# Later mixers: the third quarter of projection F right behind the scores of head step 8

## The chip, the cores and the metric

One Trainium2 chip, one core of it. The metric is the device time of one execution in microseconds (us); the median of three runs is compared. The engines have the profile's names: PE (TensorE), DVE (VectorE), ACT (ScalarE), POOL, SP. PEld is the weight load of a product.

## The reference, cut to what matters

The program computes two model blocks, one after the other, on 256 tokens of width 1024. The first is a gated linear attention, convolution and differential attention mixer with a mixture of experts. The second has two layers, each of them a feed-forward network, a token mixer and a feed-forward network:

```python
for l in range(DEPTH_2):                      # 2 layers
    x = x + 0.5 * gate0 * swiglu(h, ffn_w13[l, 0], ffn_w2[l, 0])
    x = x + gate1 * token_mixer(h, w_in[l], ..., w_out[l], cos, sin)
    x = x + 0.5 * gate2 * swiglu(h, ffn_w13[l, 1], ffn_w2[l, 1])

# token_mixer: proj = h @ w_in; three mixers of 64-wide heads, joined, @ w_out
s_cmp = einsum('bgrsd,bgcd->bgrsc', qg, kcmp) * scale     # 15 compressed keys, 8 heads
p_cmp = masked_softmax(s_cmp, cmp_mask)
o_cmp = einsum('bgrsc,bgcd->bgrsd', p_cmp, vcmp)
o     = g[..., 0:1] * o_cmp + g[..., 1:2] * o_slc + g[..., 2:3] * o_win   # heads 0 to 7
p     = masked_softmax(s + forget bias, causal)            # heads of the forgetting mixer
```

The change touches the token mixer alone, and so it acts twice in one execution, in layer 0 and in layer 1.

## The kernel before

Each engine runs a list of instructions that is written out by hand (`mixer_pe`, `mixer_act`, `mixer_dve`, `mixer_sp`, `mixer_pool`). There is no scheduler: an engine takes its list in order, and a `wait_ge` holds everything that stands behind it on that engine. Each engine has one counter; `done(key)` raises it and remembers the count, and `wait_ge(*P(key))` waits until PE's counter has that count (A is ACT's, V is DVE's).

**Projections.** The mixer's input projection is cut into blocks A to F. A block has two halves of the inner dimension (weight units `u(x, half)`) and two tiles of 128 tokens. `chunk(x, half, t)` is one quarter of a block, 12 products of 512 columns (L544, L545, L550) into bank 6 + t of `ps`. The order of the quarters is (0,0), (0,1), (1,0), (1,1), so `chunk("F", 1, 0)` is the third: the second half of the weights, on the first tile of tokens. It waits for the upper parts `whi` of its unit (ACT, L337) and the lower parts `wlo` (DVE, L344). `ahead_act(n0 + k)` and `ahead_dve(n0 + k)` make the parts of unit n0 + k + 3; block F's second half is unit n0 + 15, which `ahead_act(n0 + 12)` and `ahead_dve(n0 + 12)` make.

**Head steps.** Twelve steps `g` of two heads each go through the same stations: `scores(g)` on PE (L2473, L2483, in steps 8 and 9 L2479 too), `maxima(g)` on DVE (L2890, L2891, L2893), `exps(g)` on ACT (L2711), `norm(g)` on both (DVE L2902/L2903 or L2905, then L2909; ACT L2721), `turned_probs(g)` on PE (six transposes, L2491), `probs(g)` on both (ACT L2732, DVE L2915), `values(g)` on PE (L2503), and `emit(g)` on DVE (L2924). "The ninth head step" is g = 8.

**Compressed attention.** Its keys `KC` come from DVE (L3039, L3042). PE multiplies them with the queries in eight small f32 products of 32 columns (L2627, sixteen rows in the trace; key `cs`) into bank 5. DVE then masks (L3052), takes maxima and subtracts (L3055 to L3057), ACT takes the exponential (L2834), DVE sums and divides (L3065 to L3070, key `cp`), and PE turns the result (L2639).

On DVE, behind the scores of step 8, stand in this order: `maxima(8)`, `probs(7)`, the wait for `cs` with L3052 to L3057, `norm(8)`, `ahead_dve(n0 + 14)` (one L344), `emit(7)`, `maxima(9)`, `probs(8)`, L3065 to L3070. On ACT: `exps(8)`, `probs(7)`, `norm(8)`, L2834, `ahead_act(n0 + 15)`, `exps(9)`.

Of the kernel before, what the change touches and what calls it, by code (L numbers as in the profile page):

```python
# [140 lines left out]
class Kernel:  # L141
# [2233 lines left out]
    def mixer_pe(self, pe, l):  # L2375
# [5 lines left out]
        def chunk(x, half, t, free=None):  # L2381

            if half == 0:
                pe.wait_ge(*free)
            mm = self.proj_mm(pe, st, u(x, half), half, t, ps[:, 6 + t, 0:512], 512, False)
            if t == 1:
                mm.then_inc(*P.done("unit", u(x, half)))
                P.at["pj", st, x, 1] = P.n
            elif half == 1:
                mm.then_inc(*P.done("pj", st, x, 0))  # L2390
# [73 lines left out]
        def scores(g):  # L2464
            r = g % 2
            if g >= 2:
                pe.wait_ge(*A("pc", st, g - 2))
                pe.wait_ge(*V("pc", st, g - 2))
            heads = [self.mixer_heads(g, i) for i in range(2)]
            fox = g in (8, 9)  # L2470
            for qt in range(2):
                for i, (q, k, _) in enumerate(heads):
                    pe.matmul(ps[:, 2 * r + i, 128 * qt:128 + 256 * qt], q(qt), k(qt + 1), start=qt == 0, stop=False)  # L2473
            if fox:
                pe.wait_ge(*self.G("nFb", st))
                for qt in range(2):
                    for i in range(2):
                        h = 32 * (2 * (g - 8) + i)
                        pe.matmul(ps[:, 2 * r + i, 128 * qt:128 + 256 * qt], self.oneb[h:h + 3],  # L2479
                                  self.nFb[h:h + 3, 0:128 + 128 * qt], start=False, stop=False)  # L2480
            for i in range(2):
                for c in (0, 256):
                    mm = pe.matmul(ps[:, 2 * r + i, c:c + 128], self.identb, self.trib, start=False, stop=c == 256)  # L2483
            mm.then_inc(*P.done("sc", st, g))

        def turned_probs(g):
            r = g % 2
            for i in range(2):
                pe.wait_ge(*(A if i == 0 else V)("an", st, g))
                for c in range(3):  # L2490
                    mm = pe.transpose(ps[:, 2 * r + i, c * 128:c * 128 + 128], self.apb[:, r, i, c * 128:c * 128 + 128], ident)  # L2491
                mm.then_inc(*P.done("pt", st, g, i))

        def values(g):
            r = g % 2
            pt = self.apt[:, r, :, :]
            if g >= 1:
                pe.wait_ge(*V("em", st, g - 1))
            pe.wait_ge(*A("pc", st, g))
            pe.wait_ge(*V("pc", st, g))  # L2500
            for t in range(2):
                for i in range(2):
                    mm = pe.matmul(ps[64 * i:64 * i + 64, 4, 128 * t:256], self.mixer_heads(g, i)[2](t), pt[:, i, 256 * t:256 + 128 * t],  # L2503
                                   start=t == 0, stop=t == 1)
            mm.then_inc(*P.done("pv", st, g))
# [114 lines left out]
        values(6)  # L2620

        scores(8)
        pe.wait_ge(*V("KC", st))
        for t in range(2):
            for j in range(4):
# [1 line left out]
                mm = pe.matmul(ps[:, 5, 32 * (4 * t + j):32 * (4 * t + j) + 32], pj[:, t, c:c + 128],  # L2627
                               v["KC"].rearrange("p g c -> p (g c)"), start=True, stop=True)
        mm.then_inc(*P.done("cs", st))
        turned_probs(7)  # L2630
        chunk("F", 1, 0)
        values(7)

        scores(9)
# [758 lines left out]
```

## Time and profile before

| | |
|---|---|
| median of 3 runs | 1444.89 us (1444.31 to 1445.31) |
| profiled execution: its time, and its span | 1444.9 us, 1444.9 us |
| PE busy | 1397.9 us, 97% of the span |
| DVE busy | 1150.0 us, 80% |
| ACT busy | 791.6 us, 55% |
| the changed place, layer 0 | about 679 to 694 us |
| the changed place, layer 1 | about 1203 to 1217 us |

Span and time are the same here, so a time worked out in the trace stands for the measured one. PEclk in the rows below is the clock that TensorE was granted, as a share of 2.4 GHz: 0.50 is 1.2 GHz. A row of the timeline gives start, duration to the end of the last instruction of the group, engine, line, operation, tiles, shape and count, and in square brackets the engine's idle time before it with what ended it. Products are pipelined, so the step from one row's start to the next row's start tells more than a row's duration.

### The profile page before, as it was taken

Reading aid. Unit: us, or ns where it says so; the run is one execution under the profiler, and the core shown is the slowest. Engines: PE = TensorE matmul, PEld = TensorE weight load, DVE = VectorE, ACT = ScalarE, POOL = GpSimd, SP = SyncE. Lnnn points to the kernel's source line nnn. Section 1 sums busy time; section 2 is a strip of 40 time slices with the busy share of each in tenths; the row PEclk is TensorE's granted clock in tenths of the full one; section 3 lists DMA queues with packets and bytes.
Section 4 is the critical chain, followed back from the end, with each engine's and each line's share of the span. In section 5 each row is a group of like instructions: output and inputs, shape, how many; then the busy total and the mean of one; then the engine's idle time right before and its main releaser. Section 6 shows DMA issues by size and latency. Waiting matters only on the chain. (4 is left out here: it accounts for less than half of the span.)

```text
span 1444.9 us, 20189 instructions
## 1 busy us (share of the span) xinstructions
PE 1397.9 (97%) x7974; PEld 1188.8 (82%) x7974; DVE 1150.0 (80%) x1605; ACT 791.6 (55%) x1163; POOL 38.1 (3%) x47
## 2 busy tenths in 40 slices
PE   8998999999999999998999999999999989999997
PEld 6886888998788888777788888888888777888886
DVE  6797788889789987877778987898888787777653
ACT  7546545764456542767565543555535667655541
POOL 0021000000000000100000000000000100000000
PEclk9999999999999999999999999999999999999999
DMA  9123366998666878534347869677786433376450
GB/s 361 59 88 110 132 253 254 351 368 311 236 248 250 339 284 324 199 133 164 117 158 301 336 240 345 247 292 318 283 311 259 169 137 119 118 303 221 177 202 29
DMA packets 58110, 330.34 MB, mean 229 GB/s; under 512 B 6752, under 2 KB 7312, under 8 KB 28560
## 3 DMA queue, kind: packets, MB, share of 16 engines
q1 hardware_dynamic: 56400, 325.93, 59.8%
q10 hardware_dynamic: 1616, 3.12, 0.6%
q8 instruction: 64, 1.05, 0.3%
q14 instruction: 30, 0.25, 0.0%
HBM read 327.95 MB, written 1.07 MB: 228 GB/s over the span
## 5 line engine op out<-in xcount | busy, mean ns | idle before, releaser
L344 DVE TENSOR_TENSOR wlo<-raw,whi 128x2048 fp32r<-128x2048 f32 (+2 forms) x236 | 533.8, 2265 | 87.9 <-ACT whi L337 86.7
L337 ACT ACTIVATE whi<-raw 128x2048 fp32r<-128x2048 f32 (+2 forms) x236 | 445.9, 1894 | 134.7 <-PE ps L1622 87.5
L1374 PE MATMUL ps<-hreg_r,whi 128*128 128x512 f32 x1504 | 359.5, 391 | 1.9 <-ACT whi L337 0.8
L1374 PEld LDWEIGHTS ps<-hreg_r,whi 128*128 128x128 f32 x1504 | 276.6, 188 | 56.4 <-ACT whi L337 1.0
L385 DVE CUSTOM_DVE_ANT_0 adaw<-adaw,crow,colp 128x1024 f32<-128x1024 f32 x144 | 182.5, 1280 | 39.7 <-DMA adaw<-in_wada 39.4
L1383 PEld LDWEIGHTS ps<-hreg_r,wlo 128*128 128x128 f32 x1504 | 192.5, 191 | 7.0
L1383 PE MATMUL ps<-hreg_r,wlo 128*128 128x256 f32 x1504 | 195.6, 283 | 0.0
L1551 ACT ACTIVATE mix<-ps 128x512 f32<-128x512 f32 x93 | 55.6, 598 | 213.6 <-PE ps L1383 213.6
L1614 PE MATMUL ps<-whi,ireg_r 128*128 128x512 f32 x416 | 129.5, 392 | 1.1 <-ACT ireg_r L1508 1.1
L1618 PE MATMUL ps<-wlo,ireg_r 128*128 128x512 f32 x416 | 128.2, 389 | 0.0
L1622 PE MATMUL ps<-whi,ireg_r 128*128 128x512 f32 x416 | 128.2, 389 | 0.0
L544 PE MATMUL ps<-whi,hreg_r 128*128 128x512 f32 (+2 forms) x288 | 114.4, 401 | 3.0 <-ACT whi L337 1.3
L545 PE MATMUL ps<-whi,hreg_r 128*128 128x512 f32 (+2 forms) x288 | 108.7, 382 | 0.0
L1557 DVE TENSOR_TENSOR mix<-ps,mix 128x512 f32<-128x512 f32 x93 | 64.2, 690 | 51.2 <-ACT mix L1551 50.1
L1622 PEld LDWEIGHTS ps<-whi,ireg_r 128*128 128x128 f32 x416 | 78.0, 188 | 16.5 <-DVE ireg_r L1562 0.2
L1618 PEld LDWEIGHTS ps<-wlo,ireg_r 128*128 128x128 f32 x416 | 78.1, 188 | 16.3
L1614 PEld LDWEIGHTS ps<-whi,ireg_r 128*128 128x128 f32 x416 | 77.1, 188 | 17.1 <-ACT ireg_r L1508 1.8
L550 PE MATMUL ps<-wlo,hreg_r 128*128 128x512 f32 (+2 forms) x288 | 73.6, 378 | 0.4 <-DVE wlo L344 0.4
L544 PEld LDWEIGHTS ps<-whi,hreg_r 128*128 128x128 f32 x288 | 55.1, 191 | 14.2 <-ACT hreg_r L479 2.9
L2711 ACT ACTIVATE ireg<-ps,an 128x128 f32<-128x128 f32 x96 | 39.1, 419 | 43.1 <-DVE an L2893 43.1
L545 PEld LDWEIGHTS ps<-whi,hreg_r 128*128 128x128 f32 x288 | 55.2, 192 | 8.5
L550 PEld LDWEIGHTS ps<-wlo,hreg_r 128*128 128x128 f32 x288 | 52.5, 190 | 11.7 <-DVE wlo L344 1.7
(416 smaller groups left out, 1740.6 us busy)
## 6 DMA issues: line engine op xcount, KB each, us to landing
raw<-in_wu SPq DMA_DIRECT2D x182, 1024.0 KB, 5.8
adaw<-in_wada SPq DMA_DIRECT2D x144, 512.0 KB, 5.1
raw<-in_wx SPq DMA_DIRECT2D x48, 1024.0 KB, 6.2
greg<-gates SPq DMA_DIRECT2D x6, 512.0 KB, 6.7
raw<-in_wu SPq DMA_DIRECT2D x4, 568.0 KB, 5.9
raw<-in_wu SPq DMA_DIRECT2D x2, 544.0 KB, 5.3
x<-in_x SPq DMA_DIRECT2D x2, 512.0 KB, 4.2
out<-hreg SPq DMA_DIRECT2D x2, 512.0 KB, 2.6
```

Of the source, the lines that this page charges most:

```text
L337: act.activation(self.whi[:, m, 0:width], self.raw[:, n % NRAW, 0:width], ACT.Copy).then_inc(*self.A.done("hi", n))
L344: dve.tensor_tensor(self.wlo[:, m, 0:width], self.raw[:, n % NRAW, 0:width], self.whi[:, m, 0:width].bitcast(F32), ALU.subtract).then_inc( ...
L385: dve.tensor_tensor_reduce(w, w, self.crow, 1.0, self.col("bada")[:, n:n + 1], ALU.mult, ALU.add, self.mod2[:, n:n + 1]).then_inc(*self.V. ...
L544: pe.matmul(bank, self.hhi[:, kt, tk], wh, start=kt == 0, stop=False)
L545: pe.matmul(bank, self.hlo[:, kt, tk], wh, start=False, stop=False)
L550: mm = pe.matmul(bank, self.hhi[:, kt, tk], self.wlo[:, m, i * width:i * width + width], start=False, stop=kt == 7)
L1374: pe.matmul(self.ps[:, b, :], self.whi[:, m, c:c + 128], self.hboth[:, kt], start=kt == 0, stop=False)
L1383: mm = pe.matmul(self.ps[:, b, 0:256], self.wlo[:, m, c:c + 128], self.hhi[:, kt, :], start=False, stop=kt == 7)
L1557: dve.tensor_tensor(to, self.ps[:, b:b + 2, 0:256], to, ALU.add).then_inc(*self.V.done("sum", st, nth, part))
L1614: pe.matmul(self.ps[:, b, :], hidden(k, t)[0], weights(self.whi, k), start=first and k == 0, stop=False)
L1618: pe.matmul(self.ps[:, b, :], hidden(k, t)[0], weights(self.wlo, k), start=False, stop=False)
L1622: mm = pe.matmul(self.ps[:, b, :], hidden(k, t)[1], weights(self.whi, k), start=False, stop=last and k == 1)
```

## The change

`chunk("F", 1, 0)` and `turned_probs(7)` are written ahead of the wait for `KC` and the eight small products, where they stood behind them; among themselves they change places too.

```diff
         scores(8)
+        chunk("F", 1, 0)
+        turned_probs(7)
         pe.wait_ge(*V("KC", st))
         for t in range(2):
             for j in range(4):
                 c = MIXC["B"][0] + 128 * j
                 mm = pe.matmul(ps[:, 5, ...], pj[:, t, c:c + 128],
                                v["KC"].rearrange("p g c -> p (g c)"), start=True, stop=True)
         mm.then_inc(*P.done("cs", st))
-        turned_probs(7)
-        chunk("F", 1, 0)
         values(7)
 
         scores(9)
```

The order on PE, as a difference of the two programs (minus: before, plus: after; layer 0). First the place behind the scores of step 8 (L2479, L2483), with the small products L2627 and the transposes L2491 that leave it, and the first rows of the F quarter (L544, L545).

```order
 L2479 MATMUL ps<-nFb,greg_b 128x256 x2
 L2483 MATMUL ps<-bm 128x128 x4
-L2627 MATMUL ps<-rs,ireg 128x32 [waits dve_result]
-L2627 MATMUL ps<-rs,ireg 128x32 x7
-L2491 MATMUL ps<-cst,ireg 128x128 [waits act_result]
-L2491 MATMUL ps<-cst,ireg 128x128 x2
-L2491 MATMUL ps<-cst,ireg 128x128 [waits dve_result]
-L2491 MATMUL ps<-cst,ireg 128x128 x2
 L544 MATMUL ps<-whi,hreg_r 128x512 [waits act_result]
 L545 MATMUL ps<-whi,hreg_r 128x512
```

The F quarter now follows the scores with nothing between. Next the place behind the F quarter (its last rows are L550) and ahead of `values(7)` (L2503); the small products are L2629 in the changed file.

```order
 L550 MATMUL ps<-wlo,hreg_r 128x512 [waits dve_result]
 L550 MATMUL ps<-wlo,hreg_r 128x512 x3
+L2491 MATMUL ps<-cst,ireg 128x128 [waits act_result]
+L2491 MATMUL ps<-cst,ireg 128x128 x2
+L2491 MATMUL ps<-cst,ireg 128x128 [waits dve_result]
+L2491 MATMUL ps<-cst,ireg 128x128 x2
+L2629 MATMUL ps<-rs,ireg 128x32 [waits dve_result]
+L2629 MATMUL ps<-rs,ireg 128x32 x7
 L2503 MATMUL ps<-ireg 64x256 [waits dve_result,act_result]
 L2503 MATMUL ps<-ireg 64x256
```

The transposes of step 7 come first there, and the small products last. The lists of DVE, ACT, POOL and SP are the same in both programs. This is DVE's list at the same place, from `probs(7)` to `maxima(9)`:

```order
L2915 COPY ireg<-ps 128x384 [waits pe_result]
L3052 TENSOR_TENSOR hreg<-ps,cst 128x128 [waits pe_result]
L3052 TENSOR_TENSOR hreg<-ps,cst 128x128
L3055 TENSOR_REDUCE st<-hreg 128x16 [waits dve_result]
L3056 TENSOR_SCALAR st<-st 128x16 [waits dve_result]
L3057 TENSOR_TENSOR hreg<-hreg,st 128x256 [waits dve_result]
L2905 RECIPROCAL an<-an 128x4 [waits act_result]
L2909 TENSOR_SCALAR ireg<-ireg,an 128x128 [waits dve_result]
L2909 TENSOR_SCALAR ireg<-ireg,an 128x256
L344 TENSOR_TENSOR wlo<-raw,whi 128x2048 [waits act_result]
L2924 TENSOR_TENSOR mix<-ps,mix 128x256 [waits dve_result,pe_result]
L2890 TENSOR_REDUCE an<-ps 128x2 [waits pe_result]
```

Nothing moved in it: L3052 still waits for the small products, and everything down to L2890 still stands behind L3052.

## Rows read from the trace of the kernel before

**Rows 1.** The page's list of engines: busy time, share of the span, instructions.

```profile
PE 1397.9 (97%) x7974; PEld 1188.8 (82%) x7974; DVE 1150.0 (80%) x1605; ACT 791.6 (55%) x1163; POOL 38.1 (3%) x47
```

**Rows 2.** Windows: stretch, length, busy times, PEclk, DMA share, GB/s; both layers.

```profile
677.80:681.20 3.40, 2.86 (x31) 2.08 (x27) 3.30 (x11) 2.67 (x11) 0.00 (x0) 1.00 0.65 214
681.20:688.00 6.80, 6.80 (x24) 5.83 (x24) 4.97 (x13) 5.50 (x14) 0.00 (x0) 0.50 0.27 112
...
1203.40:1206.80 3.40, 2.86 (x26) 2.69 (x24) 2.88 (x11) 2.67 (x5) 0.00 (x0) 1.00 0.82 279
1206.80:1210.20 3.40, 3.40 (x9) 2.62 (x8) 3.26 (x10) 3.35 (x14) 0.00 (x0) 0.50 0.09 34
```

**Rows 3.** Timeline of PE, layer 0, from the scores of step 8 to L2639.

```profile
679.06 0.40 PE L2483 MATMUL ps<-bm 128*128 128x128 bf16 x4
679.99 2.57 PE L2627 MATMUL ps<-rs,ireg 128*128 128x32 f32 x16 [0.54 <-DVE ireg L3042]
682.37 1.52 PE L2491 MATMUL ps<-cst,ireg 128*128 128x128 f32 x6
...
688.54 0.87 PE L2503 MATMUL ps<-ireg 128*64 128x256 f32 x8
...
690.46 0.40 PE L2483 MATMUL ps<-bm 128*128 128x128 bf16 x4
690.70 0.82 PE L2491 MATMUL ps<-cst,ireg 128*128 128x128 f32 x6
691.28 0.48 PE L544 MATMUL ps<-whi,hreg_r 128*128 128x512 f32 x1
...
694.14 0.44 PE L2639 MATMUL ps<-cst,hreg 128*128 128x128 f32 x2
```

**Rows 4.** Timeline of DVE, layer 0, the same place.

```profile
672.49 2.29 DVE L344 TENSOR_TENSOR wlo<-raw,whi 128x2048 fp32r<-128x2048 f32 x1 [2.75 <-ACT whi L337]
...
679.18 0.76 DVE L3042 TENSOR_TENSOR ireg<-ps,cst 128x256 f32<-128x256 f32 x2
...
680.25 0.55 DVE L2909 TENSOR_SCALAR ireg<-ireg,an 128x128 f32<-128x128 f32 x2
...
683.93 0.56 DVE L2915 COPY ireg<-ps 128x384 f32<-128x384 f32 x1 [1.66 <-PE ps L2491]
684.40 0.48 DVE L3052 TENSOR_TENSOR hreg<-ps,cst 128x128 f32<-128x128 f32 x2
...
685.93 0.17 DVE L2905 RECIPROCAL an<-an 128x4 f32<-128x4 f32 x1
...
686.60 2.28 DVE L344 TENSOR_TENSOR wlo<-raw,whi 128x2048 fp32r<-128x2048 f32 x1
689.45 0.42 DVE L2924 TENSOR_TENSOR mix<-ps,mix 128x256 f32<-128x256 f32 x1 [0.57 <-PE ps L2503]
690.90 0.42 DVE L2890 TENSOR_REDUCE an<-ps 128x2 f32<-128x256 f32 x1 [1.02 <-PE ps L2483]
...
693.66 0.42 DVE L3070 TENSOR_TENSOR hreg<-hreg,st 128x256 f32<-128x256 f32 x1
```

**Rows 5.** Timeline of ACT, layer 0: norm(7), probs(7), norm(8).

```profile
680.25 0.80 ACT L2721 ACTIVATE ireg<-ireg,an 128x128 f32<-128x128 f32 x2 [0.72 <-DVE an L2903]
...
684.35 0.49 ACT L2732 ACTIVATE ireg<-ps 128x384 f32<-128x384 f32 x1
686.13 0.80 ACT L2721 ACTIVATE ireg<-ireg,an 128x128 f32<-128x128 f32 x2 [1.30 <-DVE an L2905]
```

**Rows 6.** Timeline of PE, layer 1, the same place.

```profile
1204.10 1.97 PE L2627 MATMUL ps<-rs,ireg 128*128 128x32 f32 x16 [0.54 <-DVE ireg L3042]
1205.90 0.85 PE L2491 MATMUL ps<-cst,ireg 128*128 128x128 f32 x6
...
1211.03 0.87 PE L2503 MATMUL ps<-ireg 128*64 128x256 f32 x8
...
1216.63 0.44 PE L2639 MATMUL ps<-cst,hreg 128*128 128x128 f32 x2
```

## The prediction

> **What bounds the kernel now.** I read the page's list of engines first: PE is busy 97% of the span [rows 1], so time is to be won where PE stands still, or where it runs slowly while busy. The windows show both at the changed place [rows 2]. From 681.2 to 688.0 us (layer 0) and from 1206.8 to 1210.2 us (layer 1) PE is busy all the time, but at a granted clock of 0.50, that is 1.2 GHz instead of 2.4. In the stretch ahead of each fall PE is busy 2.86 of 3.40 us. The timeline of PE says with what [rows 3]: it stands 0.54 us for the keys KC (DVE L3042, which ends at 679.18 + 0.76 = 679.94), and then issues sixteen small products (L2627). Layer 1 does the same [rows 6].
>
> The timelines of DVE and ACT then say what the place is waiting for once PE is faster [rows 4, 5]. DVE idles 1.66 us ahead of probs(7) (L2915) and 1.02 us ahead of maxima(9) (L2890), both for PE. Thus DVE has slack, but as a sum only 2.7 us in layer 0, and most of it stands ahead of L3052, which waits for the small products.
>
> **The change, step by step, layer 0.** All starts are issue times; a step is the distance of two starts.
>
> PE leaves the scores of step 8 at 679.30: L2483 starts at 679.06, and from L2483 to the next group it takes 690.70 - 690.46 = 0.24 us [rows 3]. Before, L2627 started at 679.99, so 0.69 us of standing goes. What hides the wait for KC now is the F quarter itself: 2.86 us at the full clock (691.28 to 694.14, the fourth quarter of F, same shape [rows 3]). If that cover were gone, the wait would be the old one.
>
> The F quarter needs its weights. The L344 that makes their lower parts ends at 672.49 + 2.29 = 674.78, and it waited for the upper parts [rows 4]: no wait at 679.30. It costs nothing new. It runs 679.30 to 682.16.
>
> The transposes of step 7 follow at 682.16. Their inputs are ready: ACT's half at 680.25 + 0.80 = 681.05, DVE's at 680.25 + 0.55 = 680.80 [rows 4, 5]. They take 691.28 - 690.70 = 0.58 us at the full clock [rows 3], so they issue until 682.74; before, they issued at 682.37 at the low clock.
>
> The small products issue from 682.74. At the full clock they take 1205.90 - 1204.10 = 1.80 us and end 1.97 us behind their start [rows 6]: issue until 684.54, end at 684.71. Their other bound is 2.38 us (679.99 to 682.37), part of it at the low clock [rows 3]. I take 1.80, because a solid F quarter now precedes them; the other end would make everything behind later by 0.6 us.
>
> Here the late step appears. DVE's L3052 waits for them. Before, it started at 684.40 directly behind probs(7). Now probs(7) can start at about 683.0 and is no hindrance, but L3052 starts at 684.75: **0.35 us later**. From L3052 the DVE list is fixed, steps from the rows [rows 4]: L2905 1.53 later at 686.28, L344 2.20 later at 686.95, end 2.28 on at 689.23. emit(7) (L2924) lasts 0.42 us, of which the next group overlaps some 0.1, as behind L2915 (0.56 long, next start 0.47 later). So maxima(9) starts at 689.5 instead of 690.90. Then L3070 ends (693.66 + 0.42) - 690.90 = 3.18 us behind it, at 692.7, and L2639 on PE can start at 692.73 (before 694.14, 0.06 behind L3070).
>
> PE meanwhile: values(7) waits for ACT's probs(7), 684.35 + 0.49 = 684.84 [rows 5], which the move does not make earlier: the row shows no idle time ahead of it, so ACT is busy until then. It starts at 684.88: **0.34 us of waiting**. From values(7) to the transposes of step 8 it takes 690.70 - 688.54 = 2.16 us [rows 3]: 687.04. They wait for norm(8): ACT starts 0.20 behind L2905 and takes 0.80 [rows 4, 5], so 687.28 and a start at 687.33: **0.29 us**. Transposes 0.58, fourth F quarter 2.86: PE is done at 690.77 and waits for L3070 until 692.73: **1.96 us**. Scores 9 end near 687.2 (684.88 + 690.46 - 688.54 + 0.40), long before 689.5, so DVE's list decides, with its L344 of 2.28 us inside.
>
> The sum on PE to L2639: saved are 0.69 (the wait) and the low clock's price. Transposes and F quarter took 688.54 - 682.37 = 6.17 us and need 694.14 - 690.70 = 3.44 at the full clock, 2.73 saved; the small products 2.38 - 1.80 = 0.58. Together 4.00 us. Given back are 0.34 + 0.29 + 1.96 = 2.59 us. **Layer 0: 1.4 us faster.** DVE's chain gives the same: maxima(9) 690.90 to 689.5.
>
> **Layer 1.** The old time is better there, since the low clock lasted only 3.4 us [rows 2]: small products already 1.80, transposes and F quarter 1211.03 - 1205.90 = 5.13 instead of 3.44 [rows 6]. Saved: 0.70 + 1.69 = 2.39. Given back: the same 2.59, because the DVE list is the same. **Layer 1: 0.2 us slower.** In absolute starts, L2639 moves from 1216.63 by -1.4 (layer 0's gain ahead of it) and +0.2, to about 1215.4 [rows 6].
>
> Behind L2639 the order of all lists is the old one and DVE, ACT and PE are shifted alike, so nothing is won or lost until the clock says so. No DMA is issued by the moved rows. Weight parts from `ahead_dve(n0 + 14)` are finished 0.35 us later (layer 0), and they serve a later unit.
>
> Sum: -1.4 + 0.2 = -1.2 us against the profiled execution's 1444.9, which equals the median 1444.89: **1443.7 us**.
>
> **The clock, the large unknown.** The rows show what the low clock costs: 2.73 + 0.58 = 3.3 us where it lasted 6.8 us, 1.7 us where it lasted 3.4 [rows 2, 3, 6]. They show what PE did ahead of a fall: a wait, then small products. The changed order has such places too: small products at 682.7 followed by 0.34 us of waiting, and, worse, the wait of 1.96 us ahead of L2639 followed by small groups (turns, scores). The Trainium skill ("TensorE: Matmul & The Clock Gate", section "Part 1: The HAM clock gate") says that the throttled clock is the default and that activity releases it. By that rule the new wait of about 2 us ahead of L2639 calls for a fall just behind it; the trace agrees in so far as both falls here follow a wait. By the rule the sum would be 1445.4, by the rows' full clock 1443.7.
>
> **The rivals.**
> - Forecast, clock stays full behind the change, DVE's list decides: 1443.7, own range 1443.0 to 1444.5 (0.6 us for the bound of the small products, and the spread of the runs). Chance 0.50.
> - The fall moves instead of vanishing: in one layer the low clock comes behind L2639. For it: the wait grows from nothing to 2 us. Against: two thirds of the place before it is now dense (F quarters). Price 1.7 us (short) or 3.3 us (long): 1445.4 or 1447.0. Chance 0.30, most of it short.
> - No net effect: values(7), norm(8) and the DVE list give all of the gain back, or the small products run at the low clock in both layers (1.2 us): 1444.9. Chance 0.10.
> - Slower: the clock falls behind L2639 in both layers and stays low for the long stretch, 2 x 3.3 = 6.6 us on top: 1450.3. It decides only if the falls together cost over 4.1 us, so one long fall is not enough. Chance 0.06.
> - Faster: the DVE list is not what PE waits for, because L344 or L3052 finds its place earlier, so nothing is given back: 4.0 + 2.4 = 6.4 us, 1438.5. Against it stands the fixed order of DVE. Chance 0.04.
>
> **How the numbers follow.** About 0.2% (2.9 us) is what a measurement here tells from no change. Faster than 1442.0 needs the last case, 0.04. Slower than 1447.8 needs the fourth, 0.06. The rest, 0.90, is within. The range 1443.0 to 1446.5 holds the forecast, the case without effect and the short fall, about 0.8.
>
> **What the changed profile would show.** Right: no idle time of PE ahead of the F quarter behind step 8, its start near 679.3 and its length 2.9 us at a clock of 1.00; L3052 at 684.7; PE waits for DVE L3070 about 2 us ahead of L2639; L2639 near 692.7 in layer 0 and near 1215.4 in layer 1. Wrong: a low clock in 691 to 702 or 1214 to 1225, small products of more than 2 us, or maxima(9) that starts directly behind the scores of step 9.

## The result: slower by 0.2%, outside the range

| | median us | lowest to highest | runs |
|---|---|---|---|
| before | 1445.38 | 1443.19 to 1448.60 | 16 |
| changed | 1449.09 | 1445.69 to 1453.55 | 16 |

The ratio is 1.002, 95% interval 1.0012 to 1.0029: 2.9 us slower, 1.7 to 4.2. The medians themselves lie 3.7 us apart. The forecast was 1443.7 us, with a range of 1443.0 to 1446.5 and a chance of 0.90 for no change beyond 0.2%. A second set of twelve runs of the changed kernel (label e12_after_again, below) gave 1.0017 (1.0006 to 1.0028). Single runs of either kernel differ by 5 to 8 us, which the three runs shown before did not tell. Two runs of the kernel before in one group of the experiments, at 3540 us, are left out of every ratio and mean.

The page's list of engines of the changed kernel answers to [rows 1]; nothing in it tells of the loss.

```profile
PE 1399.0 (97%) x7974; PEld 1190.2 (82%) x7974; DVE 1149.2 (79%) x1605; ACT 790.6 (55%) x1163; POOL 38.1 (3%) x47
```

PE's timeline of the changed kernel, layer 0, answers to [rows 3] (L2629 are the small products). I add L2479, the forgetting part of the scores, as a fixed point: it marks the scores of step 8 in every kernel here. The last row, L456, is the first transpose of the stage behind the mixer.

```profile
678.87 0.34 PE L2479 MATMUL ps<-nFb,greg_b 3*128 3x128 bf16 x4
...
679.35 0.48 PE L544 MATMUL ps<-whi,hreg_r 128*128 128x512 f32 x1
...
682.21 0.81 PE L2491 MATMUL ps<-cst,ireg 128*128 128x128 f32 x6
682.86 1.87 PE L2629 MATMUL ps<-rs,ireg 128*128 128x32 f32 x16
...
687.35 0.88 PE L2491 MATMUL ps<-cst,ireg 128*128 128x128 f32 x6 [0.37 <-ACT ireg L2721]
...
692.72 0.44 PE L2639 MATMUL ps<-cst,hreg 128*128 128x128 f32 x2 [1.76 <-DVE hreg L3070]
...
724.64 1.03 PE L456 MATMUL ps<-cst,hreg 128*128 128x128 f32 x8
```

DVE's timeline of the changed kernel, same place, answers to [rows 4]:

```profile
683.06 0.56 DVE L2915 COPY ireg<-ps 128x384 f32<-128x384 f32 x1 [1.69 <-PE ps L2491]
684.76 0.49 DVE L3052 TENSOR_TENSOR hreg<-ps,cst 128x128 f32<-128x128 f32 x2 [1.15 <-PE ps L2629]
...
686.29 0.17 DVE L2905 RECIPROCAL an<-an 128x4 f32<-128x4 f32 x1
...
686.96 2.28 DVE L344 TENSOR_TENSOR wlo<-raw,whi 128x2048 fp32r<-128x2048 f32 x1
...
689.50 0.41 DVE L2890 TENSOR_REDUCE an<-ps 128x2 f32<-128x256 f32 x1
```

In layer 0 each of these steps stands within 0.15 us of its forecast: the F quarter at 679.35 (679.30), L3052 at 684.76 (684.75), maxima(9) at 689.50 (689.5), L2639 at 692.72 (692.73). In layer 1 the interval from L2479 to L2639 is the same:

```profile
1205.43 0.34 PE L2479 MATMUL ps<-nFb,greg_b 3*128 3x128 bf16 x4
...
1219.28 0.44 PE L2639 MATMUL ps<-cst,hreg 128*128 128x128 f32 x2 [1.76 <-DVE hreg L3070]
```

So 13.85 us in both layers. L2639 of layer 1 was forecast at 1215.4 and stands at 1219.28, 3.9 us later, though the interval is as forecast: the time is lost between the two places. Set beside the first profile of the kernel before, the span is 2.6 us longer (1447.5 against 1444.9): -1.50 us at the place of layer 0, +1.57 behind it (30.35 became 31.92, with the low clock shown below), +2.39 from L456 to L2479 of layer 1 (1202.89 - 724.49 = 478.40 became 1205.43 - 724.64 = 480.79), +0.11 at the place of layer 1, and under 0.1 in each other part. The forecast had nothing for the second and the third of these. What it also lacked is what the unchanged place takes when the clock is full there. The windows of the changed kernel, to be read like [rows 2], show that low clock did not leave:

```profile
659.70:666.50 6.80, 6.11 (x32) 4.86 (x33) 6.59 (x8) 3.93 (x11) 0.00 (x0) 0.50 0.41 154
679.30:692.70 13.40, 11.29 (x80) 8.88 (x78) 10.18 (x28) 9.46 (x25) 0.00 (x0) 1.00 0.37 136
693.90:697.20 3.30, 3.30 (x20) 2.26 (x18) 1.78 (x5) 0.93 (x3) 0.00 (x0) 0.50 0.00 0
```

The changed place itself has the full clock, PE is busy 11.29 of 13.40 us of it, and right behind the new wait the clock is at 1.2 GHz for 3.4 us.

### The profile page after: what moved, and what is told of

Same layout as the page of the kernel before. It is cut to its first block and busy times, and to the rows that moved or that the text cites. A ratio compares the mean times of both kernels' runs of the same rounds, so it can differ in the third digit from the quotient of the medians.

```text
span 1447.5 us, 20189 instructions
## 1 busy us (share of the span) xinstructions
PE 1399.0 (97%) x7974; PEld 1190.2 (82%) x7974; DVE 1149.2 (79%) x1605; ACT 790.6 (55%) x1163; POOL 38.1 (3%) x47
## 3 DMA queue, kind: packets, MB, share of 16 engines
HBM read 327.95 MB, written 1.07 MB: 227 GB/s over the span
## 5 line engine op out<-in xcount | busy, mean ns | idle before, releaser
L344 DVE TENSOR_TENSOR wlo<-raw,whi 128x2048 fp32r<-128x2048 f32 (+2 forms) x236 | 533.4, 2264 | 89.1 <-ACT whi L337 88.0
L544 PE MATMUL ps<-whi,hreg_r 128*128 128x512 f32 (+2 forms) x288 | 112.8, 396 | 3.2 <-ACT whi L337 1.8
L545 PE MATMUL ps<-whi,hreg_r 128*128 128x512 f32 (+2 forms) x288 | 106.9, 375 | 0.0
L550 PE MATMUL ps<-wlo,hreg_r 128*128 128x512 f32 (+2 forms) x288 | 73.0, 375 | 0.4 <-DVE wlo L344 0.4
L544 PEld LDWEIGHTS ps<-whi,hreg_r 128*128 128x128 f32 x288 | 54.2, 188 | 14.2 <-ACT hreg_r L479 2.6
L550 PEld LDWEIGHTS ps<-wlo,hreg_r 128*128 128x128 f32 x288 | 51.7, 188 | 11.4 <-DVE wlo L344 1.7
L545 PEld LDWEIGHTS ps<-whi,hreg_r 128*128 128x128 f32 x288 | 54.2, 188 | 8.2
```

The lines of the kernel that those rows point to most:

```text
L344: dve.tensor_tensor(self.wlo[:, m, 0:width], self.raw[:, n % NRAW, 0:width], self.whi[:, m, 0:width].bitcast(F32), ALU.subtract).then_inc( ...
L544: pe.matmul(bank, self.hhi[:, kt, tk], wh, start=kt == 0, stop=False)
L545: pe.matmul(bank, self.hlo[:, kt, tk], wh, start=False, stop=False)
L550: mm = pe.matmul(bank, self.hhi[:, kt, tk], self.wlo[:, m, i * width:i * width + width], start=False, stop=kt == 7)
```

## The experiments

Three theories. **List**: the small products come later, DVE's fixed list (L3052 to L3057, norm(8), L344, maxima(9), L3070) starts later, and PE waits for its end in each layer. **Clock**: the new wait brings low clock behind it. **DMA**: the loss arises in the later feed-forward stages. Each kernel had 11 or 12 runs. They ran in three groups (e1 to e4, e5 to e8, e9 to e12), each on one chip of its own, and a ratio is taken against the 35 runs of the kernel before on the same chip, whose medians were 1445.9, 1445.9 and 1444.3 us. So across groups the ratios are to be compared, not the medians. The table below is worked out from each profile's starts: L2639 minus L2479 of step 8 (the place), L456 minus L2639 (what is behind it in the mixer). For the first profile of the kernel before, the rows of PE that [rows 3, 6] lack are these, the first for layer 0 and the last for layer 1, and they give 694.14 - 678.79 = 15.35, 724.49 - 694.14 = 30.35 and 1216.63 - 1202.89 = 13.74:

```profile
678.79 0.34 PE L2479 MATMUL ps<-nFb,greg_b 3*128 3x128 bf16 x4
...
724.49 1.03 PE L456 MATMUL ps<-cst,hreg 128*128 128x128 f32 x8
...
1202.89 0.34 PE L2479 MATMUL ps<-nFb,greg_b 3*128 3x128 bf16 x4
```

| kernel | median us | ratio (95%) | place, layers 0 and 1 | behind, layers 0 and 1 |
|---|---|---|---|---|
| before, first profile | 1445.38 | | 15.35, 13.74 | 30.35, 30.37 |
| e5 before again | 1445.04 | 0.9997 (0.9984 to 1.0009) | 13.75, 11.59 | 30.33, 30.33 |
| changed | 1449.09 | 1.0020 (1.0012 to 1.0029) | 13.85, 13.85 | 31.92, 30.32 |
| e12 changed again | 1447.91 | 1.0017 (1.0006 to 1.0028) | 13.85, 13.86 | 30.34, 31.89 |
| e8 layer 0 alone | 1447.37 | 1.0012 (1.0000 to 1.0024) | 13.85, 11.59 | 30.36, 30.36 |
| e1 L344 moved | 1446.58 | 1.0007 (0.9995 to 1.0018) | 11.96, 11.95 | 31.89, 31.89 |
| e6 before, L344 moved | 1448.10 | 1.0016 (1.0005 to 1.0027) | 12.16, 12.16 | 32.04, 33.29 |
| e2 wait filled | 1446.88 | 1.0015 (1.0001 to 1.0028) | 13.86, 13.87 | 30.32, 30.35 |
| e3 transposes last | 1448.42 | 1.0014 (1.0002 to 1.0025) | 14.36, 14.36 | 30.36, 30.36 |
| e10 norm(8) first | 1446.64 | 1.0016 (1.0003 to 1.0029) | 13.67, 13.66 | 31.92, 31.68 |
| e4 F quarter split | 1443.57 | 0.9991 (0.9977 to 1.0005) | 12.51, 12.51 | 30.34, 30.33 |
| e11 the same again | 1445.09 | 0.9994 (0.9981 to 1.0008) | 12.52, 12.52 | 30.36, 30.32 |
| e7 split, L344 moved | 1446.24 | 0.9999 (0.9986 to 1.0012) | 11.77, 11.77 | 32.08, 32.04 |
| e9 before, wait filled | 1445.31 | 0.9997 (0.9986 to 1.0008) | 12.33, 12.33 | 30.36, 30.33 |

**e5, the kernel before again.** No edit.

> The kernel before, unchanged, for a second profile and more runs. In the first profile both layers had low clock at the changed place. Theory List says what it looks like where a layer has the full clock there: small products 1.8 us, PE at L2639 about 11.1 to 11.5 us behind the start of the small products (it was 14.15 and 12.53 us with the low clock), and 1.3 to 1.7 us ahead of the same point of the changed kernel, measured from the scores of step 8. Theory Clock alone says that a layer at the full clock is no faster to L2639 than the changed kernel's.

Its PE timeline of layer 1 is the unchanged order at the full clock:

```profile
1203.31 0.34 PE L2479 MATMUL ps<-nFb,greg_b 3*128 3x128 bf16 x4
1203.82 1.92 PE L2627 MATMUL ps<-rs,ireg 128*128 128x32 f32 x16
...
1214.90 0.44 PE L2639 MATMUL ps<-cst,hreg 128*128 128x128 f32 x2
```

and DVE's:

```profile
1206.94 0.48 DVE L3052 TENSOR_TENSOR hreg<-ps,cst 128x128 f32<-128x128 f32 x2
...
1209.13 2.29 DVE L344 TENSOR_TENSOR wlo<-raw,whi 128x2048 fp32r<-128x2048 f32 x1
...
1211.67 0.42 DVE L2890 TENSOR_REDUCE an<-ps 128x2 f32<-128x256 f32 x1
```

L3052 starts 3.63 us behind L2479; in the changed kernel 684.76 - 678.87 = 5.89. That is 2.26 us, and L2639 is late by the same: 13.85 against 11.59. So the direction is List's, with a larger size than expected (1.3 to 1.7). One reason is that this layer did not even wait for KC: L2627 follows L2479 by 0.51 us, where a wait makes it 1.20 (679.99 - 678.79). The windows of this profile show what may have made PE late enough not to wait:

```profile
682.40:685.80 3.40, 3.40 (x12) 2.83 (x11) 2.50 (x10) 3.02 (x12) 0.00 (x0) 0.50 0.26 106
1184.30:1191.00 6.70, 6.00 (x32) 4.76 (x31) 6.62 (x8) 3.80 (x11) 0.00 (x0) 0.50 0.42 157
1203.30:1214.90 11.60, 11.56 (x87) 8.96 (x85) 10.54 (x30) 9.47 (x25) 0.00 (x0) 1.00 0.48 157
```

Low clock stood some 19 us ahead (1184.3 to 1191.0). That PE came late from there, and so found KC ready, is my reading; e8's layer 1, with no wait either, has 11.59 us too, and the same stretch 19 us ahead of its L2479 at 1201.91:

```profile
1182.80:1189.60 6.80, 6.05 (x32) 4.80 (x31) 6.67 (x8) 3.84 (x11) 0.00 (x0) 0.50 0.45 152
```

So the two intervals of 11.59 us are not free of low clock: its price was paid ahead of L2479, where the table does not count it. An unchanged layer at the full clock that does wait for KC takes longer, as e9 shows below. Layer 0 of e5 had its low clock at the place (682.4), 13.75 us. Where low clock falls changes between runs of one kernel.

**e1 and e6, L344 out of the list.** The same edit on DVE, in the changed kernel and in the kernel before:

```diff
         norm(8)
-        self.ahead_dve(dve, n0 + 14)
 
         emit(7)
         maxima(9)
...
         dve.tensor_tensor(S16, S16, sm..., ALU.mult).then_inc(*V.done("cp", st))
+        self.ahead_dve(dve, n0 + 14)
```

> The changed kernel, with one thing moved: on DVE the L344 that stands between norm(8) and emit(7) comes behind L3070. Theory List: the small products, late by the F quarter, hold L3052 and everything behind it on DVE, and with the 2.28 us of L344 in that list PE waits 1.8 us ahead of L2639 in each layer. Then L2639 comes near 690.9 in layer 0 (692.72 in the changed kernel), the wait ahead of it is under 0.3 us, and the median is 3 to 4 us under the changed kernel's, 1445 to 1446. Theory Clock: what costs is low clock behind that wait. It expects the same direction, as the wait is gone, but with the low clock gone from behind L2639. Theory DMA (the loss arises in the later feed-forward stages, from landings of weights that come at another time): no gain, 1448 to 1450.

> The kernel before, with L344 moved behind L3070 on DVE, as in the experiment on the changed kernel. Theory List: before the change PE hardly waits ahead of L2639, so there is nothing to win: within 1 us of the kernel before, 1445 to 1447. A rival says that the moved L344 alone makes the kernel faster, with or without the change: then 1442 to 1444.

PE of e1, layer 0:

```profile
678.74 0.34 PE L2479 MATMUL ps<-nFb,greg_b 3*128 3x128 bf16 x4
...
690.70 0.38 PE L2639 MATMUL ps<-cst,hreg 128*128 128x128 f32 x2
693.64 0.87 PE L2491 MATMUL ps<-cst,ireg 128*128 128x128 f32 x6 [1.07 <-ACT ireg L2721]
```

The wait ahead of L2639 is gone and the place takes 11.96 us, 1.9 less, as List says: DVE's list set the 13.85. But the stretch behind takes 31.89 instead of 30.3 in both layers, at the full clock: L344 now holds norm(9), and PE waits for that (1.07 us ahead of the transposes of step 9). So the edit gives back most of what it wins: place and rest are 43.85 against 44.2 us. Its ratio is 1.0007 against the changed kernel's 1.0020, some 1.9 us less, more than these 0.35 us per layer; the rest may be low clock (see "The mean granted clock" below) or spread. The median, 1446.58, lies above the 1445 to 1446 expected. e6 shows the other side: in the kernel before the move takes away next to nothing and costs the same 1.7 us behind, 0.16% slower (layer 1 also has low clock behind the place, 33.29). I had expected no difference there. Its PE list is that of the kernel before, so it gives two more layers of the unchanged order on PE. Both wait for KC, and neither has low clock at the place. This is the wait in layer 0, and the window of that place:

```profile
680.49 1.97 PE L2627 MATMUL ps<-rs,ireg 128*128 128x32 f32 x16 [0.55 <-DVE ireg L3042]
```

```profile
679.30:691.40 12.10, 11.55 (x86) 8.97 (x84) 9.40 (x33) 10.16 (x29) 0.00 (x0) 1.00 0.25 91
```

**e2, the wait filled.** On PE, in the changed kernel:

```diff
         chunk("F", 1, 1)
+        for k in range(14):
+            pe.matmul(ps[:, 5, 256:512], self.hhi[:, k % 4, 0:128], self.hhi[:, k % 4, :], start=True, stop=True)
         pe.wait_ge(*V("cp", st))
```

> The changed kernel, with fourteen extra products of 256 columns (about 1.7 us at the full clock) on PE inside its wait ahead of L2639, into a free half of bank 5; their result is not used. The order and the waits stay. Theory Clock: PE never idles there, no low clock comes behind L2639, and the median falls by the share of runs that had it, 1 to 3 us, to 1446 to 1448. Theory List: L2639 stays at 692.7 in layer 0, since it waits for DVE, and only the falls go; if they were rare the median stays at 1448.5 to 1449.5. Theory DMA: no change.

```profile
691.00 1.83 PE L2638 MATMUL ps<-hreg_r 128*128 128x256 f32 x14
692.90 0.44 PE L2641 MATMUL ps<-cst,hreg 128*128 128x128 f32 x2
```

PE's idle time is gone, L2639 (here L2641) stays 13.86 us behind L2479, and no low clock stands behind it in either layer. The median, 1446.88, lies where Clock expected it (1446 to 1448) and below List's 1448.5 to 1449.5, but the ratio 1.0015 is only 0.7 us under the changed kernel's 1.0020, and the interval (1.0001 to 1.0028) overlaps it. So filling the wait leaves most of the loss in place; a share of Clock is allowed and not shown by the times.

**e3, the order of the three.** The small products ahead of `turned_probs(7)`, both behind the F quarter; against the changed kernel:

```diff
         chunk("F", 1, 0)
-        turned_probs(7)
         pe.wait_ge(*V("KC", st))
...
         mm.then_inc(*P.done("cs", st))
+        turned_probs(7)
         values(7)
```

> The F quarter ahead of the small products, but the transposes of step 7 behind them. The small products end 0.6 us earlier, but DVE's probs(7), which stands ahead of L3052, now waits until 684.7. Theory List: DVE's L3052 starts near 685.2 instead of 684.76, all behind it 0.45 us later per layer, so 0.9 us slower than the changed kernel, near 1450. Theories Clock and DMA: no difference to the changed kernel.

The small products are earlier, and L3052 is later all the same, as DVE's list says:

```profile
686.27 0.56 DVE L2915 COPY ireg<-ps 128x384 f32<-128x384 f32 x1 [2.45 <-PE ps L2491]
686.75 0.48 DVE L3052 TENSOR_TENSOR hreg<-ps,cst 128x128 f32<-128x128 f32 x2
```

L2479 stands at 680.34 in this profile, so L3052 comes 6.41 us behind it (5.89 in the changed kernel), and the place takes 14.36: 0.5 us more, as expected. The median was expected near 1450 and is 1448.42; the times cannot tell 1 us.

**e10, norm(8) ahead of L3052 on DVE.** Against the changed kernel:

```diff
         probs(7)
+        norm(8)
         dve.wait_ge(*P("cs", st))
...
         dve.tensor_tensor(S16, S16, mx..., ALU.subtract).then_inc(*V.done("cm", st))
-        norm(8)
         self.ahead_dve(dve, n0 + 14)
```

> The changed kernel with norm(8) on DVE ahead of the wait for the small products and L3052 to L3057, instead of behind them. Theory List, from the steps of the changed kernel's rows: norm(8) no longer waits for the small products, the list behind L3057 moves up by 0.67 us, L2639 comes 13.2 us behind the scores of step 8 instead of 13.86, and the median is 1.3 us lower, 1447 to 1448. If something else than DVE's order holds L2639, it stays at 13.86.

A miss: 13.67 instead of 13.2. The profile names the cause, the exps of step 8 on ACT, which held norm(8) for nearly 1 us and L3052 behind it:

```profile
685.72 0.18 DVE L2905 RECIPROCAL an<-an 128x4 f32<-128x4 f32 x1 [0.96 <-ACT ireg L2711]
...
686.40 0.48 DVE L3053 TENSOR_TENSOR hreg<-ps,cst 128x128 f32<-128x128 f32 x2
```

With exps(8) in the way the place is shorter by 0.18 us only, instead of 0.67. The median, 1446.64, is under the 1447 to 1448 expected, and the ratio (1.0016) is that of the changed kernel on the same chip (e12, 1.0017).

**e8, layer 0 alone.** `small()` holds the wait for KC and the eight products:

```diff
+        if l == 0:
+            chunk("F", 1, 0)
+            turned_probs(7)
+            small()
+        else:
+            small()
+            turned_probs(7)
+            chunk("F", 1, 0)
```

> The change in layer 0 alone, layer 1 as before. Theory List and theory Clock: half of the change's 2.6 us in the mean, so 1446.5 to 1448. Theory DMA (the loss arises in the stages behind layer 0's mixer): all of the loss or none of it, 1448 to 1449.5 or under 1446.5.

Both orders in one profile:

```profile
677.69 0.34 PE L2479 MATMUL ps<-nFb,greg_b 3*128 3x128 bf16 x4
...
691.54 0.44 PE L2648 MATMUL ps<-cst,hreg 128*128 128x128 f32 x2 [1.73 <-DVE hreg L3079]
```

```profile
1201.91 0.34 PE L2479 MATMUL ps<-nFb,greg_b 3*128 3x128 bf16 x4
...
1213.50 0.44 PE L2648 MATMUL ps<-cst,hreg 128*128 128x128 f32 x2
```

13.85 against 11.59 us, and the ratio 1.0012 is a little over half of the change's 1.0020. The cost sits in each layer, as List says; the intervals are too wide to exclude a share of theory DMA. Low clock of 6.8 us, 19 us ahead of layer 1's place, belongs to the 11.59.

**e4, e11 and e7, the F quarter split.** Four of its twelve products ahead of the small ones, eight behind the transposes (e7 with L344 moved as well):

```diff
         scores(8)
+        self.proj_mm(pe, st, u("F", 1), 1, 0, ps[:, 6, 0:512], 512, False, part=0)
         pe.wait_ge(*V("KC", st))
...
         turned_probs(7)
-        chunk("F", 1, 0)
+        self.proj_mm(pe, st, u("F", 1), 1, 0, ps[:, 6, 0:512], 512, False, part=1)\
+            .then_inc(*P.done("pj", st, "F", 0))
```

> Only the first four products of the F quarter (0.9 us) stand ahead of the small products, just enough to cover the wait for KC; then the small products, the transposes of step 7, and the other eight. Theory List: L3052 starts near 683.3, L2639 near 691.2 with at most 0.8 us of waiting, 1.5 us per layer less than the changed kernel: median 1445 to 1446.5, level with the kernel before. Theory Clock: a gain only as far as low clock goes, with no wait of 1.8 us left to cause it. Theory DMA: no gain, 1448 to 1450.

> The kernel with four products of the F quarter ahead of the small ones, once more, for its interval and a second profile: the median was 1443.57. If it is really better than the kernel before, it stays at 1443 to 1445, below the kernel before of the same chip; if the first result was luck of the runs, 1445 to 1446.5. L2639 12.5 us behind the scores of step 8 where the clock is full.

> Four products of the F quarter ahead of the small ones, and L344 behind L3070: both orders together. Theory List: the wait ahead of L2639 that the split kernel still has (0.64 us) goes, another 0.6 us per layer: 1442 to 1443.5. If PE is the bound already, 1443.5 to 1444.5.

PE of e4, layer 0:

```profile
679.91 0.48 PE L544 MATMUL ps<-whi,hreg_r 128*128 128x512 f32 x1
...
680.93 1.87 PE L2630 MATMUL ps<-rs,ireg 128*128 128x32 f32 x16
...
691.95 0.44 PE L2643 MATMUL ps<-cst,hreg 128*128 128x128 f32 x2 [0.64 <-DVE hreg L3074]
```

The same cover for the wait, with the small products 1.49 instead of 3.99 us behind L2479: the place takes 12.51 us, 1.35 less than in the changed kernel, and all four layers had the full clock at it. The ratios are 0.9991 and 0.9994: under the changed kernel's 1.0020 and 1.0017, and not shown to beat the kernel before, since both intervals reach over 1. The second set came out as I had expected it for luck in the first: its median of 1445.09 is above the 1444.3 of the kernel before on the same chip. e7 wins 0.74 us more at the place and loses 1.7 behind it, like e1 and e6; its median, 1446.24, lies outside what was expected.

**e9 and e12.** e9 is the kernel before with its wait for KC filled by products that add zeros:

```diff
         scores(8)
+        for k in range(12):
+            pe.matmul(ps[:, 7, 0:128], self.identb, self.trib[:, 0:1].to_broadcast([128, 128]), start=False, stop=False)
```

> The kernel before, with its wait for KC (0.5 us) filled by twelve extra bf16 products of 128 columns (about 0.67 us) that add zeros to bank 7. Nothing is moved. In the profiles of the kernel before, 3 of 5 unchanged layers had low clock right behind the small products, at a price of 1.5 to 3 us. If the wait helps to cause it, low clock leaves the changed place, L2639 comes 12.2 to 12.5 us behind the scores of step 8 in both layers, and the mean falls by 1 to 3 us, to 1443 to 1445. If the small products alone cause it, the low clock stays and the median is that of the kernel before.

> The changed kernel, once more, for a second profile: which stretches it has at low clock, and whether L2639 comes 13.86 us behind the scores of step 8 in both layers again. Theory List: yes, in both layers, whatever the clock did before. Median 1447.5 to 1449.5.

PE of e9, layer 0:

```profile
677.90 0.34 PE L2479 MATMUL ps<-nFb,greg_b 3*128 3x128 bf16 x4
678.40 0.85 PE L2624 MATMUL ps<-bm 128*128 128x128 bf16 x12
679.10 1.97 PE L2629 MATMUL ps<-rs,ireg 128*128 128x32 f32 x16
...
690.23 0.44 PE L2641 MATMUL ps<-cst,hreg 128*128 128x128 f32 x2
```

and its first row of L3052, which is L3054 in this file:

```profile
682.28 0.48 DVE L3054 TENSOR_TENSOR hreg<-ps,cst 128x128 f32<-128x128 f32 x2
```

In e9's profile no low clock is at the place (12.33 us in both layers, against 13.75, 13.74 and 15.35), though the small products are the old ones. That the filling did this is not shown by the profile, since e6, with the wait open, had none there either. The times do not follow: the ratio is 0.9997, and the mean of 1444.45 is 0.4 us under the mean of the kernel before on that chip (1444.82), where I expected 1 to 3.

e9 is also the cleanest measure of List. Its small products start 1.20 us behind L2479, where the wait for KC puts them in the kernel before too, and the clock is full: the unchanged order without the low clock and without the luck of coming late. Its L3052 comes 682.28 - 677.90 = 4.38 us behind L2479 (e6 has 4.39), the changed kernel's 5.89: 1.51 us later. Its L2639 comes after 12.33 us, the changed kernel's after 13.85: 1.52 later. So the lateness of the small products reaches PE whole, and the size is the 1.3 to 1.7 us expected. e12 has 13.85 and 13.86 us at the place again, and low clock behind it in the other layer (31.89), as its windows say:

```profile
1207.00:1220.80 13.80, 11.76 (x86) 9.19 (x84) 11.50 (x34) 10.16 (x29) 0.00 (x0) 1.00 0.40 137
1221.70:1225.00 3.30, 3.30 (x18) 2.11 (x18) 2.07 (x5) 1.22 (x3) 0.00 (x0) 0.50 0.00 0
```

**The mean granted clock.** A profile shows one execution, but every run has its mean granted clock on record. A stretch at 1.2 GHz costs about half of its length (3.3 us for 6.8, 1.7 for 3.4, from the rows of the prediction), so 0.001 of this mean is worth about 1.4 us, an estimate from those rows.

| kernel | runs | mean granted clock | standard error |
|---|---|---|---|
| before, all three chips | 103 | 0.9936 | 0.0002 |
| changed, with e12 | 28 | 0.9934 | 0.0004 |
| e1 L344 moved | 11 | 0.9943 | 0.0004 |
| e2 wait filled | 12 | 0.9948 | 0.0006 |
| e4 and e11, quarter split | 24 | 0.9948 | 0.0003 |
| e9 before, wait filled | 12 | 0.9949 | 0.0003 |

The change left the total of low clock as it was: the difference is 0.3 us of time, with a standard error of 0.6. So Clock carries at most about 1.5 of the 2.9 us, and probably little. Where a wait was filled or made short the mean is higher, by 0.0011 to 0.0014, worth some 1.6 to 2.0 us; for e2 that is only two standard errors. The split kernel owes part of its time to it: by these means some 2 us of what it is faster than the changed kernel is low clock, beside the 1.35 us per layer of its order.

## Why the prediction was wrong

**Right, step by step.** The interval from L2479 to L2639 in both layers: it was to become 1.4 us shorter and 0.2 us longer than in the first profile, and became 1.50 shorter and 0.11 longer. The cover for the wait, the readiness of the weights, the lateness of L3052 against the small products, the role of L344 in the list, L2639 at 692.7 and the wait ahead of it (1.76 us and the last product's own end; 1.96 forecast). ACT's values(7) wait (0.34) did not come in layer 0, since ACT was 0.9 us earlier in that run; it hardly mattered.

The recorded sign of being wrong, low clock in 691 to 702, came true in layer 0 (693.9).

**The step that failed** is "saved are 0.69 (the wait) and the low clock's price", 4.0 us in layer 0 and 2.4 in layer 1. Of these, 3.3 and 1.7 us are low clock. The sum took the place of the low clock in one profiled execution for a property of the kernel before. It is not: of five unchanged layers in the profiles (the first profile, e5, and layer 1 of e8), three had it at the place and two had it 19 us ahead, and the two layers of e6, with the unchanged list on PE, had none at the place. Nor did the change take it away: the mean granted clock is 0.9936 before and 0.9934 after. What is given back is paid in every layer; what is saved at the place comes back, in the mean, at another.

Without that credit the prediction's own terms come near the result. Saved is the wait, 0.69 us; given back are 2.59 us, or 2.25 without the 0.34 us that did not come: 1.56 us slower in each layer, against 1.52 measured (13.85 against e9's 12.33). Against that measure L3052 is late by 1.51 us, where the sum, set beside a layer at low clock, had 0.35. Twice 1.52 is 3.0 us, and the whole kernel lost 2.9 (1.7 to 4.2); that the two agree does not show that nothing else counts, as the term below tells.

The table gives a second way to the size, and it is weaker. Unchanged layers: the mean of 15.35, 13.74, 13.75, 11.59 and 11.59 is 13.20 us at the place, and 30.35 behind. Changed layers (two profiles, and layer 0 of e8): 13.85 at the place and 31.92, 30.32, 30.36, 30.34 and 31.89 behind, mean 30.97. The difference is 0.65 + 0.62 = 1.3 us per layer, 2.6 for both. That this too is near 2.9 is partly luck: it counts low clock at and behind the place, but not the stretches ahead of it (1184.2 in e5, 1182.8 in e8, 659.7 in the changed kernel). Its two shares are not a result.

**A term put at nothing.** "Behind L2639 the order of all lists is the old one" and "nothing is won or lost until the clock says so" failed in the profiles. In the profile of the changed kernel PE waits 1.88 us in the feed-forward stage behind the mixer of layer 0, and in e12 again; in the first profile of the kernel before it does not:

```profile
914.06 1.09 PE L456 MATMUL ps<-cst,hreg 128*128 128x128 f32 x8 [1.88 <-DVE hreg L436]
```

```profile
915.13 1.09 PE L456 MATMUL ps<-cst,hreg 128*128 128x128 f32 x8 [1.16 <-DVE hreg L436]
```

```profile
911.91 1.03 PE L456 MATMUL ps<-cst,hreg 128*128 128x128 f32 x8
```

DVE was late there, behind landings of the weights `adaw`; the last one ahead of L436 in the profile of the changed kernel:

```profile
905.76 1.28 DVE L385 CUSTOM_DVE_ANT_0 adaw<-adaw,crow,colp 128x1024 f32<-128x1024 f32 x1 [1.53 <-DMA adaw<-in_wada]
```

The same wait stands in the profiles of e1 (1.06 us), e2 (0.40), e3 (0.80) and e10 (0.49): in all six of the kernels that have the whole quarter ahead in both layers, and in none of the other eight. From L456 of layer 0 to L2479 of layer 1 these six take 479.7 to 481.4 us; the split kernels take 477.8 to 479.3, the kernel before in its first profile, e6 and e9 take 478.2 to 478.4, and e5 and e8 take 480.2 and 480.0 with 6.8 us of low clock inside. This is theory DMA, and it speaks for a share of it. Against it: e8 has the changed order in layer 0, ahead of this stage, and does not have the wait. Why the landings are later was not tried, and no run separates this wait from List in the times. With List's 3.0 us it would make more than the 2.9 measured, so how the loss divides stays open.

**The base of the sum.** The section on the time before says that span and time are the same. In every run whose time and span are both given, the time is 1.8 to 1.9 us above the span (1449.29 and 1447.5 for the changed kernel). So the first profile, with a span of 1444.9, was probably an execution of some 1446.7 us, 1.3 slower than the median of 1445.38. It was not unusual in its amount of low clock (0.993, near the mean of 0.9936), only in having it at the place in both layers.

**The rivals.** "The fall moves instead of vanishing" was the nearest: it did, in two of five changed layers, at 1.6 us each (the price given was 1.7). But low clock moved among the executions of the kernel before as well, and the forecast it was added to was too low, and its times (1445.4, 1447.0) are below the measured one. No rival said that the list alone makes the place longer than it is before at the full clock. The rule of the Trainium skill ("TensorE: Matmul & The Clock Gate", section "Part 1: The HAM clock gate"), activity releases the throttle, pointed the right way as a tendency: in e2, with the wait filled, low clock stood behind neither layer, and with a wait filled the mean granted clock was 0.9948 (e2) and 0.9949 (e9). It did not hold in each execution: low clock came behind the new wait in two of five changed layers, and e6 has the wait for KC in both layers with no low clock behind it at the place.

**Open.** Why the landings at 905 us come later with the whole quarter ahead, what share the wait behind them has in the loss, and what decides where the low clock falls.

## What to carry to other kernels

A wait of PE can be covered with less work than stands ready: put ahead of it only as much as the wait is long, since all that is behind the delayed result on another engine's fixed list moves too (0.9 us of products covered the wait as well as 2.9 us did, and cost 1.35 us less per layer). Before counting a stretch of low clock as a saving, see whether a second execution of the same kernel has it at the same place, and compare the mean granted clock of many runs of both kernels: it tells whether low clock went or only moved. And a long weight split on DVE belongs where neither chain waits: moving it from one to the other cost 1.6 to 1.7 us behind the place (31.9 and 32.0 against 30.3).

## What the runs showed of the hardware

Low clock comes at different places in executions of one program: in the kernel before at 681.2 and 1206.8 us in one profile, at 682.4 and 1184.3 in the other; in the changed kernel at 659.7 and 693.9 in one, and in the other (e12) only at 1221.7 of these stages. The stretches last 3.4 or 6.8 us. Others come at nearly the same place: all 14 profiles have one that starts between 117 and 123 us, and nine have one between 390 and 396. Over 103 runs of the kernel before the mean granted clock is 0.9936, some 9 us of time per execution (an estimate, half of the length of the stretches). The same single steps are repeated to 0.02 us between executions (13.85, 13.85, 13.85, 13.86), while the scores of step 8 in layer 0, ahead of which nothing was changed, start anywhere from 677.69 (e8) to 682.22 us (e12).
